# Placing every operand of the three-fold products at byte 128 within 256

## The reference, cut to what matters

```python
def swiglu(h, w_gu, w_d):
    g, u = jnp.split(h @ w_gu, 2, axis=-1)
    return (jax.nn.silu(g) * u) @ w_d
```

```python
    d_intra = jnp.exp(log_gamma[:, None, None] * dist)
    scores = jnp.einsum('bhncd,bhnmd->bhncm', qc, kc) * d_intra[None, :, None]
```

## Time and profile before

| | |
|---|---|
| median of 3 runs | 1857.26 us (1856.21 to 1858.22) |
| the profiled execution | 1859.97 us, of which the span of its instructions 1858.1 us |
| PE busy | 1818.2 us (98%), 12,229 matmuls and as many weight loads |
| DVE busy, ACT busy | 1341.6 us (72%), 950.0 us (51%) |
| granted TensorE clock, mean | 0.993 |
| DMA | 383 MB, mean 206 GB/s |

### The profile page before, as it was taken

The page is one execution under the profiler, slowest core; times in us unless marked ns, Lnnn a source line. Parts: engine busy times, 40 slices in busy tenths (PEclk is TensorE's granted clock), DMA queues, the critical chain, the costliest instruction groups (busy, mean ns, idle before and its releaser), DMA issues.

```text
span 1858.1 us, 31832 instructions
## 1 busy us (share of the span) xinstructions
PE 1818.2 (98%) x12229; PEld 1599.1 (86%) x12229; DVE 1341.6 (72%) x1986; ACT 950.0 (51%) x1504; POOL 0.2 (0%) x4
## 2 busy tenths in 40 slices
PE   7999999999999999999999999999999989999997
PEld 5777777776878999999999999999998966777786
DVE  5888999985777776677667676677777663337797
ACT  4334765754346654465446554455455452336685
POOL 0000000000000000000000000000000000000000
PEclk9999999999999999999999999999999989999999
DMA  9957997995411476666666466666646446779894
GB/s 321 293 180 223 307 287 224 299 297 159 119 46 47 132 206 178 182 181 188 178 187 184 117 193 178 182 182 181 165 128 184 125 161 250 283 283 360 300 365 195
DMA packets 516045, 383.23 MB, mean 206 GB/s; under 512 B 13769, under 2 KB 473170, under 8 KB 515794
## 3 DMA queue, kind: packets, MB, share of 16 engines
q1 hardware_dynamic: 515408, 381.25, 66.2%
q10 hardware_dynamic: 514, 0.30, 0.1%
HBM read 380.45 MB, written 1.05 MB: 205 GB/s over the span
## 4 chain that ended last, share of the span: by engine, by line
PE 93%; DVE 3%; ACT 2%; issue 1%; DMA 1%; ACTq 0%; SPq 0%; DVEq 0%
PE ps L2620 19%; PE ps L2621 19%; PE ps L2622 18%; PE ps L3376 3%; PE ps L3377 3%; PE ps L3378 3%; PE ps L2633 2%; PE ps L2635 2%; PE ps L2634 2%; PE ps L3404 2%; PE ps L3406 2%; PE ps L3405 2%; PE ps L3392 2%; PE ps L2706 1%; PE ps L3028 1%
## 5 line engine op out<-in xcount | busy, mean ns | idle before, releaser
L2620 PE MATMUL ps<-nhi,hi 128*128 128x258 f32 (+2 forms) x1904 | 581.4, 305 | 0.0
L2621 PE MATMUL ps<-nlo,hi 128*128 128x258 f32 (+2 forms) x1904 | 578.7, 304 | 0.0
L2622 PE MATMUL ps<-nhi,lo 128*128 128x258 f32 (+2 forms) x1904 | 577.6, 303 | 0.0
L1638 DVE TENSOR_TENSOR lo<-raw,hi 128x1024 fp32r<-128x1024 f32 (+2 forms) x387 | 459.2, 1188 | 107.1 <-ACT hi L1088 106.1
L1088 ACT ACTIVATE hi<-raw 128x1024 fp32r<-128x1024 f32 (+2 forms) x388 | 395.4, 1023 | 231.0 <-PE ps L2622 172.7
L2620 PEld LDWEIGHTS ps<-nhi,hi 128*128 128x128 f32 x1904 | 359.7, 189 | 25.5 <-issue 7.2
L2622 PEld LDWEIGHTS ps<-nhi,lo 128*128 128x128 f32 x1904 | 360.4, 189 | 15.7
L2621 PEld LDWEIGHTS ps<-nlo,hi 128*128 128x128 f32 x1904 | 359.6, 189 | 15.6
L2620 PE MATMUL ps<-hhi,hi 128*128 128x256 f32 (+1 forms) x576 | 176.9, 307 | 0.0
L2622 PE MATMUL ps<-hhi,lo 128*128 128x256 f32 (+1 forms) x576 | 176.3, 306 | 0.0
L2621 PE MATMUL ps<-hlo,hi 128*128 128x256 f32 (+1 forms) x576 | 176.3, 306 | 0.0
(11 more groups left out here) (457 smaller groups left out, 2985.4 us busy)
## 6 DMA issues: line engine op xcount, KB each, us to landing
raw<-in_ffn_w_gu SPq DMA_DIRECT2D x176, 512.0 KB, 4.7
modw<-in_w_mod SPq DMA_DIRECT2D x56, 1024.0 KB, 7.4
raw<-in_ffn_w_d SPq DMA_DIRECT2D x64, 512.0 KB, 4.4
raw<-in_w_in SPq DMA_DIRECT2D x36, 512.0 KB, 4.7
raw<-in_w_exp_gate SPq DMA_DIRECT2D x32, 512.0 KB, 6.5
raw_more<-in_w_exp_gate SPq DMA_DIRECT2D x32, 512.0 KB, 7.7
raw<-in_w_exp_up SPq DMA_DIRECT2D x32, 512.0 KB, 7.6
raw_more<-in_w_exp_up SPq DMA_DIRECT2D x32, 512.0 KB, 5.6
```

Source lines behind the costliest of these rows:

```text
L1638: v.tensor_tensor(lo[:, s], raw[:, s], hi[:, s].bitcast(F32), ALU.subtract).then_inc(lo_ready, 1)
L2620: pe.matmul(bank(u, T), w_hi(u, k), h_, start=(k == 0), stop=False)
L2621: pe.matmul(bank(u, T), w_hi(u, k), l_, start=False, stop=False)
L2622: ins = pe.matmul(bank(u, T), w_lo(u, k), h_, start=False, stop=(k == nk - 1))
```

## The change

The chunks of `nhi` and `nlo` get 576 columns, 2,304 bytes, nine times 256. The buffers from `sq` on start at byte 128 within 256, and so does the shared region. The region is then 3,136 bytes further up, its layout for the second block no longer fits below the limit, and the decay tables (6,144 bytes) move out of it into the memory of `sg` and `hf`, the silu buffers (8,192 bytes). No instruction is added, removed or reordered, and no wait changes.

```diff
 DEC_W = SEQ + P
-LINE = 64
-NORM_W = BOTH + LINE // 4
+TURN, PHASE = 256, 128
+NORM_W = BOTH + TURN // 4
 SHIFT_COLS = 2
...
-        def to_line():
+        def to_phase():
 
-            place[0] = -(-place[0] // LINE) * LINE
+            place[0] += (PHASE - place[0]) % TURN
...
         rootc = sb("rootc", 1)
+        to_phase()
         sq_at = place[0]
...
         nt = sb("nt", 2 * BOTH)
+        sg_at = place[0]
         sg = sb("sg", 2 * BOTH)
         hf = sb("hf", 2 * BOTH)
-        to_line()
+        to_phase()
         region = place[0]
...
         wz = A("wz", 5 * 2 * DEC_W)
-        decay = A("decay", 4 * DEC_W)
+        assert 4 * DEC_W <= 2 * 2 * BOTH
+        decay = sb("decay", 4 * DEC_W, at=sg_at)
```

## The result

The kernel with the change takes 1861.64 us (median of 19 runs, 1859.2 to 1864.25) against 1858.04 us for the kernel before (median of 19 runs, 1855.97 to 1859.98). The ratio is 1.0019, 95% interval 1.0013 to 1.0026: slower by 3.6 us, just under what I had called the grain of a measurement, but clear of noise over 19 runs. I had forecast 1820.

A forecast was written before the change was run, and what follows sets the result against it. PE, 93% of the chain, was taken to bound the kernel by multiplying, not waiting; five `slab` terms gave 36.8 us, other parts nothing, so 1820 against the median (1823 against the profiled run), range 1809 to 1832, to 1848 with the poor lock.

The forecast's parts named there:

- a stream has a floor: PE's waitless matmul streams: anything above 226.7 ns (512 columns) or 113.3 (256) is lost; all `slab` matmuls would reach these.
- the terms of 16.3, 7.9 and 4.5: Gains in us forecast in `slab` for nhi with 258 columns, nhi with 256 and hhi with 256.
- The 258-column term: nhi in `slab`: 3,024 matmuls from 119.6 to 114.2 ns, a gain of 16.3 us; ends 114.2 and 119.6.
- a sign that the prediction is wrong: PE's timeline at `slab`: distances that keep differing from chunk to chunk, or that fall while the span does not.
- The two 512-column terms: `slab`: nhi from 231.7 to 226.7 ns, 5.5 us gained; hhi from 233.3 to 226.7, 2.6 us.
- settling after stalls: PE streams after a stall: 0.05 us each, 5 us for a hundred, left to cancel against gains at other lines.
- The up slabs: Experts' up slabs: 2.2 ns each, among other lines' 5 to 10 us, left to cancel; no gain counted with the experts.
- Decay tables and sq at nothing: Decay tables in silu buffers: cost zero, covered by 75 us; buffers from sq on: zero, within a microsecond either way.
- The poor lock: Rival in `slab`: 256 columns settle at 117.9 ns, 258 at 118.8, only 512 reach 226.7; gain 9.4 us, 1848; chance 0.17.
- The worst place made permanent: Rival, slower: 258 columns settle at 0.13 us, costing 31 us, 1868 after the others' gains; chance 0.07.
- Addresses being indifferent: Rival: distances come from what feeds a stage, not addresses; 1857, also the skill rule's time; chance 0.08.
- PE outrunning its supply in layer 0: Rival: in layer 0, 8 of the 37 us come back as waits, 1828; within the forecast's own range.

The follow-up runs named there:

- widths_at_128: Changed kernel, but the three later feed-forwards' up products take 320, 384 and 322 columns in place of 258, from byte 128 as before: 1972.9 us, one run.
- all_at_0: Changed kernel with weights, nhi and region all at byte 0 within 256, the same relative places: 1859.11 us, one run.
- nhi0_hhi192: Changed kernel with nhi and nlo at byte 0, shared region at 192, stationary weights still at 128: 1869.97 us beside 1858.52 for the kernel before, one run each.
- nhi192_hhi0: Changed kernel with nhi and nlo at byte 192, shared region at 0, stationary weights still at 128: 1854.96 us.
- decay_and_sq_only: Kernel before with only the decay tables in the silu buffers and buffers from sq on at byte 128: 1858.71 us against 1857.64, ratio 1.0004.

## Why the prediction was wrong

**The step that failed** is "a stream has a floor, 226.7 ns for 512 columns, and 113.3 ns, just half of it, for 256". The 226.7 came from equal places, the 113.3 from hhi at an offset of -64, and I joined them because one is half the other. At equal places the overhead doesn't go with the length: it is 32 cycles, 13.3 ns, per matmul at 256, 320, 384 and 512 columns (widths_at_128). So 256 columns cost 120.0 and not 113.3. That one step carried 28.7 of the 36.8 us: the terms of 16.3, 7.9 and 4.5. They came out as +3.4, +2.4 and +4.2. The 258-column term was stretched from the same number; it measured 120.8, which is 1.2 ns above the 119.6 that I gave as its upper end. I also called rows 8 and 10 the two nearest fixed-place rows; rows 7, with the same place and width as rows 8, were as near, and dearer.

**What held.** The distance of a waitless stream depends on addresses, the moving against the stationary place (all_at_0, and the up slabs of nhi0_hhi192 and nhi192_hhi0). The fixed place does let a stream of 512 or 256 columns settle, at 226.7 and 120.0 ns, the same at every chunk. With 258 columns it does not: the distances go on differing, 113 to 125 ns, which I had named as a sign that the prediction is wrong. Nor does going round the four places cost much by itself. For 258 columns the four fixed places have 120.8, 118.7, 122.2 and 120.8 ns, 120.6 in the mean, and the rotating stream had 119.7; for 512 they have 230.6 in the mean, against 231.8. The two 512-column terms came as 3.8 and 1.8 us of 5.5 and 2.6. In the first, settling after stalls (a mean of 227.4 and not 226.7) took 0.8 us of the rest, and distances with a wait took about as much. The up slabs gave 3.8 us, more than I counted. Decay tables and sq at nothing: within what is measurable (decay_and_sq_only).

**The rivals.** The poor lock was the right kind of answer: the 256-column streams do settle in a dear state. I priced it from rows 7, 117.9 ns, as if the state at -64 were the state at 0; with the measured 120.0 and 120.8 ns it would have given a loss of 2.7 us (8.1 gained at 512 columns; 3.6, 2.7 and 4.5 lost at 258, at 256 in nhi and at 256 in hhi). The worst place made permanent was right in its direction and wrong in its place: 258 columns are at 120.8 and not at 130, and it is the 256-column ones that lost most. Addresses being indifferent is refuted. By the rule of the Trainium skill ("TensorE: Matmul & The Clock Gate", "Step-by-step: what each phase is for") the load of the next stationary tile doesn't steal read bandwidth from the running matmul. From it I had concluded that a stream with the same loads keeps one distance wherever its operands lie. The runs disagree with that outcome: the same instructions take 226.7 to 234.3 ns at 512 columns and 113.3 to 120.0 at 256, with only addresses changed. Whether it is the load that does it, no run isolated. That the rival's total, no change, came nearest is an accident of two effects with opposite signs, -6.5 us by the attention and +9.4 after it. PE outrunning its supply in layer 0 showed as 0.8 us of idle time before DVE's lo, not 8, though the chain's share of PE fell to 79% where I had expected over 90%.

**What I could have read.** The rows gave a warning: at one offset, -64, hhi cost 560 cycles for 512 columns and 272 or 283 for 256. 48 cycles over at 512 and 16 or 27 at 256 shows that the overhead depends on the width, and each place could have its own such pattern; I had only 512 columns' 32 cycles at equal places. No row showed 256 columns at equal places, and I bounded that cost from one side only.

**Open.** Why equal places cost 32 cycles, what makes +64 and -64 have two states for 256 columns where one was seen for 512, and what in the entry picks the state. That the overlap of the next stationary load with the stream is the cause fits the offset rule, but no run took the load away, so it is argued and not shown.

## What to carry to other kernels

Read a tuned matmul stream by the distance from start to start, for each width by itself, and measure the placement for each width: the offset of the moving against the stationary operand that is best for 512 columns (0) is, with +96, the dearest for 256. A number taken at one width or one placement must not be scaled to another. Here the placement alone was worth 0.8% with nhi at +64 and hhi at -64, and 0.9% with hhi at 0 for its 512-column products, with no instruction added, removed or reordered.

## What the runs showed of the hardware that I had not expected

A stream of float32r matmuls, each with its own load of 128 x 128, has at equal places, at a granted clock of 1.00, a cost of columns + 32 cycles of 2.4 GHz (256, 320, 384, 512 columns: 120.0, 146.7, 173.3, 226.7 ns). At an offset of -64 or +64 bytes 256 columns can run at +16 cycles (113.3 ns) or at 117.8 to 117.9 ns, at the same addresses, and one wait in the stream can be enough to go from one to the other. At an odd multiple of 32 bytes 512 columns take 233.3 ns (offsets of +32, -32 and +96) or 234.3 (-96). And a product whose three matmuls stream from two different places (258 columns: 122.2 ns) is dearer than from either (118.7 to 119.0 and 120.8).
